# One core, two attentions: latents, the first pair, shared keys and values, and two filler counts reordered

## What is computed

```python
h = h + 0.5 * swiglu(rms(h), ...)                     # feed-forward, d_ff 2816
# layer 0: latent attention, 16 heads of 64 + 32 rotary
z = rms(h) @ w_in                                      # 384 query latents, 256 kv latents, 32 rotary key
q = rms(rope(rms(z[:, :384]) @ w_qup))                 # 16 x 96
k, v = rms([latent @ w_kvup | k_pe]), latent @ w_kvup  # over cached + new rows
h = h + softmax(q k^T, chunk-causal) v @ w_a_out
h = h + 0.5 * swiglu(rms(h), ...)
# shared keys, values and forget gates of layer 1
k, v, f = split(rms(h) @ w_kvf);  k = rms(k);  log_f = log_sigmoid(f + b_f)
h = h + 0.5 * swiglu(rms(h), ...)
# layer 1: forgetting attention, 16 heads of 64
q = rms(rms(h) @ w_b_q);  c = cumsum(log_f)
h = h + softmax(q k^T + c_q - c_k, causal) v @ w_b_out
h = h + 0.5 * swiglu(rms(h), ...);  y = rms(h)
```

## Time and profile before

| what | value |
|---|---|
| three runs | 2276.39, 2276.72, 2273.26 us (median 2276.39) |
| the profiled execution, own time | 2273.43 us |
| its span | 2271.4 us |
| mean granted clock | 0.985 |
| instructions in the span | 45624 |
| HBM | 82 GB/s over the span |

### The profile page before, as it was taken

One profiled execution on the slowest core, in us unless ns is written; L12 is line 12 of the kernel. 1 busy time (PEld: TensorE's weight loads), 2 busy tenths in 40 slices (PEclk: granted clock), 3 DMA queues, 4 the chain that ended last, 5 costly groups with the idle time before them and its releaser, 6 DMA issues.

```text
span 2271.4 us, 45624 instructions
## 1 busy us (share of the span) xinstructions
PE 2222.7 (98%) x16677; PEld 2144.9 (94%) x16677; DVE 1685.8 (74%) x2718; ACT 1087.2 (48%) x1839; POOL 308.5 (14%) x276
## 2 busy tenths in 40 slices
PE   8999999999999999999999999999999999999998
PEld 8999999988888999999978999999988899999998
DVE  7984984478886896698446995896368868966983
ACT  6542543456675553354324551453357755533541
POOL 0000002035552000000123000001134520000001
PEclk8999999999999999999999999999989999999999
DMA  3222233100002222222223322223222222222222
GB/s 116 93 101 94 93 107 102 46 26 21 15 19 75 75 104 96 87 95 104 75 90 117 113 99 95 93 93 114 73 57 51 55 74 75 102 98 87 95 99 77
DMA packets 73904, 187.60 MB, mean 83 GB/s; under 512 B 40852, under 2 KB 44388, under 8 KB 62536
## 3 DMA queue, kind: packets, MB, share of 16 engines
q1 hardware_dynamic: 72520, 181.73, 23.5%
q0 software_dynamic: 1280, 4.49, 0.6%
HBM read 178.75 MB, written 7.35 MB: 82 GB/s over the span
## 4 chain that ended last, share of the span: by engine, by line
PE 88%; DVE 5%; ACT 3%; issue 2%; DMA 0%; DVEq 0%; POOL 0%; ACTq 0%; SPq 0%
PE ps L734 21%; PE ps L668 19%; PE ps L669 18%; PE ps L670 18%; PE ps L837 6%; PE ps L1043 2%; PE ps L932 1%; PE ps L1107 1%; DVE hid_lo L2083 1%; PE ps L686 1%; PE ps L1134 1%; DVE stat L2440 1%; ACT arena L1698 1%; DVE xs_lo L2083 1%; DVE arena L2537 0%
## 5 line engine op out<-in xcount | busy, mean ns | idle before, releaser
L668 PE MATMUL ps<-xs_hi,w_hi 128*128 128x272 f32 x1408 | 409.6, 291 | 2.1 <-DVE scratch L2191 1.1
L670 PE MATMUL ps<-xs_hi,w_lo 128*128 128x272 f32 x1408 | 407.8, 290 | 0.0
L669 PE MATMUL ps<-xs_lo,w_hi 128*128 128x272 f32 x1408 | 407.1, 289 | 0.0
L1406 ACT ACTIVATE w_hi<-raw 128x1408 fp32r<-128x1408 f32 (+4 forms) x123 | 146.0, 1188 | 454.9 <-PE ps L734 224.7
L1467 ACT ACTIVATE w_hi<-w_blocks 128x1024 fp32r<-128x1024 f32 x176 | 186.8, 1061 | 308.8 <-PE ps L670 156.7
L669 PE MATMUL ps<-xs_lo,w_hi_more 128*128 128x272 f32 x1056 | 306.9, 291 | 0.0
L668 PE MATMUL ps<-xs_hi,w_hi_more 128*128 128x272 f32 x1056 | 306.5, 290 | 0.0
L668 PEld LDWEIGHTS ps<-xs_hi,w_hi 128*128 128x128 f32 x1408 | 266.4, 189 | 3.4 <-DVE w_lo_more L2109 1.3
L734 PE MATMUL ps<-hid_hi,w_hi 128*128 128x256 f32 (+1 forms) x1290 | 265.7, 287 | 1.3 <-DVE w_lo L2073 1.0
L670 PEld LDWEIGHTS ps<-xs_hi,w_lo 128*128 128x128 f32 x1408 | 266.9, 190 | 0.0
L669 PEld LDWEIGHTS ps<-xs_lo,w_hi 128*128 128x128 f32 x1408 | 266.6, 189 | 0.0
(11 more groups left out here) (315 smaller groups left out, 5044.6 us busy)
## 6 DMA issues: line engine op xcount, KB each, us to landing
w_blocks<-w_ffn_in SPq DMA_DIRECT2D x88, 1024.0 KB, 4.8
raw<-w_ffn_out SPq DMA_DIRECT2D x64, 704.0 KB, 4.1
raw<-w_b_kv SPq DMA_DIRECT2D x16, 512.0 KB, 3.2
raw<-w_a_out SPq DMA_DIRECT2D x8, 512.0 KB, 3.3
raw<-w_b_q SPq DMA_DIRECT2D x8, 512.0 KB, 3.3
raw<-w_b_out SPq DMA_DIRECT2D x8, 512.0 KB, 3.2
raw<-w_a_in SPq DMA_DIRECT2D x4, 672.0 KB, 4.1
raw<-w_a_qup SPq DMA_DIRECT2D x8, 288.0 KB, 2.8
```

The source lines that it names most:

```text
L668: pe.matmul(out, lhs[0], rhs[0], start=start, stop=False, skip_group_check=more)
L669: pe.matmul(out, lhs[0], rhs[1], start=False, stop=False, skip_group_check=more)
L670: return pe.matmul(out, lhs[1], rhs[0], start=False, stop=stop, skip_group_check=more)
L1406: act.activation(wh[par][:, 0:n], raw[par][:, 0:n], ACT.Copy).then_inc(w_hi, 1)
```

## The change

It touches six places.

1. **Latents.** The squares of the four whole query-latent tiles, their square root and the reciprocal (four columns) come ahead of the low rows and of the fifth tile, which has a square, a root and a reciprocal of its own. `turn_latents` starts when four tiles are scaled and waits for the fifth ahead of the sample turns.
2. **Weights of pair 1.** SP loads them earlier; both are split into slot 1 (`w_second` and the values' part), on ACT after `low_rows` and on DVE ahead of `cqT_lo`.
3. **First pair.** kv(1) groups 0 and 1 run ahead of q0, on banks 0 and 1; `keep_clock` there goes from 19 to 7, that of `pair_a(0)` from 15 to 4; waits for values v0 to v4 are spread over scores and turns. On ACT the table load and exp(0, 0) come earlier; on DVE the sums of pair 1's keys come after two maxima, and `norm_keys` between the q0 and q1 parts; the splits for pair 2 come later on both. POOL's `stage_values(0)` waits for the normalised queries.
4. **KV and Q.** `low_rows` (ACT) and `take_chunk` or `take_queries` (DVE) come ahead of the next weight split at m = 4, 8, 12 (Q: 4). The forget product goes to `MISC` and bank 2, and waits for the root of the row sums, and the wait of tile 5 for its copy goes.
5. **Cumulative sums.** 14 matmuls in place of 25: wider ones (64, 48, 32, 16 columns) for the tiles of each stream, five of 16 columns for the samples.
6. **Second attention.** Ahead of scores(0, 4) PE waits for the first of the last query tiles and issues `keep_clock` of 3.

```diff
-F_BANKS = [7, 2]
+SECOND_BANKS = FIRST_BANKS | {"kv0": 0, "kv1": 1}
+F_BANKS = [MISC, 2]
...
             sp.dma_start(chunk_rows, d["c_chunk_rows"]).then_inc(loaded["chunk_rows"], 16)
+            load(0, M["u"] + 2, d["w_a_qup"][1], QC * 2 * DA)
+            load(1, M["u"] + 3, d["w_a_kvup"][1], LC * 4 * DV)
...
-                        keep_clock(bank_of("t" + name, uses, before), 19, latT[0])
+                        keep_clock(bank_of("t" + name, uses, before), 7, latT[0])
...
-                        keep_clock(7, 15, latT[0])
+                        keep_clock(7, 4, latT[0])
...
-                    pe.wait_ge(*Z["st"]["dve"].at("cq4"))
-                    turn_latents(Q_OFF, QC, Q_BANKS)
+                    pe.wait_ge(*Z["st"]["dve"].at("cq3"))
+                    turn_latents(Q_OFF, QC, Q_BANKS, Z["st"]["dve"].at("cq4"))
...
-                    for name in ("p0", "p1", "c0", "c1", "q0", "q1"):
+                    for name in ("p0", "p1", "c0", "c1"):
+                        staged(name, 0, new, uses, True)
+                    project_kv(1, new, uses, range(2))
+                    for name in ("q0", "q1"):
                         staged(name, 0, new, uses, True)
...
-                    project_kv(1, new, uses)
-                    pe.wait_ge(*prk["act"].at("v4", 1))
+                    project_kv(1, new, uses, range(2, 5))
                     pair_a(0, True, True)
...
                     for u in range(5):
+                        if u == 4:
+                            pe.wait_ge(*Q["k"][1]["act"].at("c0"))
+                            keep_clock(7, 3, xa[0])
                         scores(0, u, 0)
...
-                elif n in (5, 6):
-                    pe.wait_ge(*KV["forget"]["dve"].at(f"fs{n - 5}"))
+                elif n == 6:
+                    pe.wait_ge(*KV["forget"]["dve"].at("fs1"))
...
                     pe.wait_ge(*KV["forget"]["dve"].at("wlo"))
+                    pe.wait_ge(*KV["rms"]["act"].at("sd"))
...
-                    for t in range(NK):
-                        o = ps[:, MISC, 128 + t * HEADS:128 + (t + 1) * HEADS]
-                        past = range(t) if t < 4 else range(NT, NK) if t == 4 else range(NT, t)
-                        for n, s in enumerate(past):
-                            pe.matmul(o, ones[:, :], lf[:, s, :], start=(n == 0), stop=False)
-                        r0 = S0 if t == 4 else 0
-                        mm = pe.matmul(o, tri[r0:P, :], lf[r0:P, t, :], start=len(past) == 0, stop=True)
+                    for t0 in (0, NT):
+                        pe.matmul(sums_to(t0, 4), tri[:, :], lf[:, t0:t0 + 4, :], start=True, stop=False)
+                        for back in range(1, 4):
+                            pe.matmul(sums_to(t0 + back, 4 - back), ones[:, :], lf[:, t0:t0 + 4 - back, :],
+                                      start=False, stop=back == 3)
+                    for t in range(NT, NK):
+                        pe.matmul(sums_to(4, 1), ones[:, :], lf[:, t, :], start=t == NT, stop=False)
+                    mm = pe.matmul(sums_to(4, 1), tri[S0:P, :], lf[S0:P, 4, :], start=False, stop=True)
```

More of the change, by code:

```diff
@@ L961, in turn_latents @@
                     mm.then_inc(Z["st"]["pe"].sem, 1)
+                if samples_ready is not None:
+                    pe.wait_ge(*samples_ready)
                 for j in range(n):
@@ L999, in bank_of, with project_q @@
                     return b
-                def project_q(it, uses, before, groups=range(3), ahead_of_last=None):
+                def project_q(it, uses, before, groups=range(3), ahead_of_last=None, w=None):
                     unit_ready(M["u"] + 2 * it)
+                    w = [t[0] for t in (wh, wl)] if w is None else w
                     for n in groups:
@@ L1676, in _ @@
             latents_hi("k", LC, latT[0], KEYS, SEQ + PAST, LAT_BANKS, None)
+            square_latents("sq", Q_OFF, Q_RANK, ST_MS, range(4))
             low_rows(Z, Z["u"] + 3, 1, Z_BANKS[2 * NT - 1], ZW // 2, st["dve"].at("z04"))
-            square_latents("sq", Q_OFF, Q_RANK, ST_MS)
+            u = M["u"] + 2
+            act.wait_ge(w_load[0], 16 * (u // 2 + 1))
+            act.wait_ge(w_used, Z["u"] + 3 + PRIME + 1)
+            act.activation(w_second[0], raw[0][:, 0:QC * 2 * DA], ACT.Copy).then_inc(w_hi, 1)
+            act.wait_ge(w_load[1], 16 * (u // 2 + 1))
+            act.activation(wh[1][:, 0:LC * 4 * DV], raw[1][:, 0:LC * 4 * DV], ACT.Copy).then_inc(w_hi, 1)
+            square_latents("sq", Q_OFF, Q_RANK, ST_MS, range(4, 5))
             def load_exp():
@@ L2003, in _ @@
                              None if c == 0 else KV["k"][c - 1]["dve"].at("c4"))
+                if m < 15:
+                    ahead(KV["u"] + m + 1)
                 if m == 0:
@@ L2573, in pair_a @@
                     top(1, 1, p)
+                    if first:
+                        mean_square_keys(1)
                     split_p(0, 0, p)
@@ L2586, in pair_a @@
                         stage_part("q0", p + 1)
+                        if first:
+                            norm_keys(p + 1)
                         stage_part("q1", p + 1)
                         if first:
-                            norm_keys(p + 1)
+                            split_units(2)
                         for name in ("p0", "p1", "c0", "c1"):
@@ L2928, in _ @@
             for m in range(8):
-                ahead(U + m + 1)
+                if m != 4:
+                    ahead(U + m + 1)
                 if m == 0:
```

124 lines of the change are left out of this document (73 added, 51 removed).

## The result

| | before | with the change |
|---|---|---|
| runs with the first comparison | median 2274.82 us (2268.62 to 2276.72, 4 runs) | median 2247.09 us (2244.57 to 2252.23, 4 runs) |
| ratio | | 0.9892, 95% interval 0.987 to 0.9914 |
| the profiled execution, own time | 2273.43 us | 2244.57 us |
| its span, granted clock | 2271.4 us, 0.985 | 2242.5 us, 0.993 |

The change is clearly faster, by about 28 us. Times are medians over all executions; the ratios leave out one of a2 (5480 us) and one of b1 (3077 us), far off the rest.

The account below looks back on a forecast made before the run. PE, busy 98% of the span, was taken as the bound, DMA not. Terms -9.5 (way in), -5.3 (KV and Q) and -5 (second attention) sum to -19.8 from 2273.43: 2253.6, leaned up to 2255; range 2247 to 2266.

Parts of the forecast that it names:

- Latents, -5.1: Query-latent turns: start 3.8 us earlier, and 12 turns at full clock save 1.3 more.
- First pair, q0 5.5 earlier, PE the later: First attention: q0 starts 5.5 us earlier, set by PE's products and fillers rather than by the normalised queries.
- I take -9.5 for the whole way in.: Latents through first pair, up to pair 1's keys: 9.5 us saved, ends -5.1 and -11.5.
- the 11 fillers of pair_a(0): First attention, pair_a(0): 11 of 15 fillers go, 2.6 us, about half of it counted.
- the 2.7 of the 24 products: First attention: 24 products gone from behind the scores, so the next pair's keys come another 2.7 us earlier.
- KV and Q, -5.3: KV and Q stages: waits gone at m = 4, m = 8 and in Q, shorter sums; 5.3 us saved, ends -2.4 and -6.
- Second attention, -5: Second attention's entry: fillers prevent 14 us at half clock; 5 us saved, ends 0 and -6.8.
- Slower, by clock through the first attention: Rival: cut fillers leave TensorE at 1.2 GHz through the first attention's pairs, over 0.2% slower; chance 0.03.
- the 41 at which I had it decide: First attention: half clock must last more than 41 us, at 0.49 per us, to eat the gain.

Follow-up runs that it names:

- a2: Changed kernel with the old filler numbers in the first attention (19 ahead of q0, 15 in pair_a(0)), new order kept; 2250.93 us, ratio 0.991.
- b1: Kernel before with only the latents' reordering (four query-latent tiles ahead of the fifth), no weight split moved; 2268.59 us, ratio 0.9975.
- a1: Changed kernel without the wait and three fillers ahead of scores(0, 4) of the second attention; 2246.25 us, ratio 0.9883.
- c1: Kernel before with only the KV and Q reordering, the forget product's banks and the 14-matmul sums; 2256.91 us, ratio 0.9942.
- c2: Kernel before with only the way in changed (latents, weights of pair 1, first pair); 2256.12 us, ratio 0.9945.
- c3: Changed kernel with 3 fillers in place of 7 ahead of q0 and without the second attention's entry fillers; 2247.48 us, ratio 0.9898.
- a4: Kernel before with only the wait and three fillers ahead of scores(0, 4) of the second attention added; 2268.42 us, ratio 0.9989.
- b2: Kernel before with only the first attention's fillers cut (19 to 7, 15 to 4), old order; 2272.83 us, ratio 1.0005.
- c4: The changed kernel run again, as reference and second trace; 2240.22 us, ratio 0.987.
- a3: Changed kernel with DVE's weight split ahead of take_chunk again at m = 4, 8 and 12 of KV; 2255.16 us, ratio 0.9926.

## Why the prediction was right, and where it was off

Steps in the order of the prediction, with the changed kernel's marks.

- **Latents, -5.1.** Right: -5.5, the wait gone, 12 turns in 1.48 us, the splits hidden.
- **First pair, q0 5.5 earlier, PE the later.** Right: 5.8 earlier from mark 436, the queries ready at 453.83, the fillers' end at 454.6; a2 shows PE as the later.
- **"I take -9.5 for the whole way in."** Too small: -12.8. The terms named came nearly as forecast: latents and q0 0.3 more, the 11 fillers of pair_a(0) half of their 2.6 (a2 against the changed kernel: 1.3). What was missing lies between q0 and scores(1, 0): -5.8 there where only the 2.7 of the 24 products was in the sum. The stretch at half clock at 466.40 before was in none of my terms; its going was worth 1.6. The stand of 0.68 for v4 ahead of scores(1, 0) went too, and came back behind it as the new stand of 1.30. The rest are shorter stands.
- **KV and Q, -5.3.** -6.6 measured (0.8 + 2.1 + 3.0 + 0.6), and 1.2 for the clock behind the sums, which I had left out.
- **Second attention, -5.** In this pair of traces -4.8 at the entry and -4.6 in the two pairs behind it. But a1, c1, c2 and c3 gained 2.2 to 3.7 at the entry without the fillers: the trace before showed the long kind of fall, and I priced the part by that one trace. The fall at scores(1, 0) went as forecast; that the 5 us came out is luck, and by the medians of a1 and a4 no gain of this part is clear of noise.
- **Slower, by clock through the first attention.** Did not come; b2 shows its mechanism in one trace: behind the cut two stretches of 17 us together up to 498 where before had one of 3.4, still short of the 41 at which I had it decide.

In sum, -19.8 was forecast against the profiled execution and -28.9 came. Of the 9.1 between, 3.3 are the way in, 1.3 KV and Q, 1.2 the clock behind the sums, 4.4 the second attention and 1.8 the start, less 3.0 given back near 673 and 683, and rounding. About 6 of the 9.1 are time at half clock (1.6, 1.2, 4.4 and 1.8, less 3.0), taking the start as clock too, where the trace before has stretches of 6.8 and 10.2 us and the changed one only 6.8. That the total fell inside the range is luck in part: each of the three terms of the sum was too small, and c4's series ended below it.

**Open.** Why a stretch at half clock comes in one run and not in the next near 673, 748 or 1870 isn't settled: near 673 PE stands alike in the traces with and without (1.07 and 1.06 us, then 0.94 and 0.94), and in the 12 us ahead of the stretches at 748 and 1868 it doesn't stand in either. Open too is what the fillers of the second attention are worth over many executions, and what beyond its trace makes a3 8 us slower.

## What to carry to other kernels

Filler matmuls on PE are worth replacing by real work of the next step, not by standing: the same cut of 23 fillers is worth 4 us with 24 products moved into the gap (a2), and without them it cost 4.3 at that place in the trace of b2 and gained nothing over its 12 executions. When an engine's queue holds an op that frees a buffer and one that has slack, put the freeing one first, above all where POOL's running product would hold the other (2.2 us at m = 8 in a3). A wait that is spread over several steps has to be looked for in the trace: a helper that takes the next bank may still ask for the last of them. Price a stretch at half clock from several traces, not from one: the runs of the kernel before lie up to 13 us apart.

## What the runs showed of the hardware that I had not expected

- 25 fp32 matmuls of 16 columns take 5.8 us and 14 of 16 to 64 columns 3.0: a narrow one costs 0.21 to 0.24 us on average whatever its width. Each appears twice in the trace, with two weight loads, and these fill the time: PEld is busy 5.84 of the 5.90 us of the earlier trace rows.
- Narrow matmuls didn't keep the clock here: PE was busy without a break through the sums, and the granted clock fell to 0.5 during them or as they ended in all six traces with 25 of them, and in one of eight (c4) behind 14.
- A DVE product of two SBUF inputs waits for POOL's running product and, by the times, starts about when it ends: 1.08, 1.08 and 1.09 us from POOL's end to its own, whether it was issued 0.9, 1.4 or 1.65 us ahead of that end. Copies out of PSUM aren't held: the four tiles of m = 8 took 2.73 us in the changed kernel, from 1171.40 beside POOL's product (1167.54 to 1174.20), and 2.71 before, from 1187.68 behind it.
